# Splitting fp32 weights chunk by chunk in place of half by half, in a transformer layer on one NeuronCore

## The reference, cut to what matters

```
ul = (xl * (1 + sc1_l) + sh1_l) @ w_in          # 2048 x 13824, context likewise
y  = (gated linear recurrence, mean pooling, windowed attention)(uc, ul)
z  = sum over 3 branches of sigmoid(gates) * (y_j @ w_branch_j)
xl = layer_norm(ALPHA * xl + g1 * (z @ w_out))
xl = layer_norm(ALPHA * xl + g2 * (square(relu(mod(xl) @ w_ff1)) @ w_ff2))
```

## Time and profile before

| | |
|---|---|
| median of 3 runs | 1952.09 us (1946.99 to 1952.15) |
| profiled execution, whole | 1952.81 us |
| its span, first to last instruction | 1951.0 us |
| PE busy | 1885.7 us, 97% |
| DVE busy | 1258.3 us, 64% |
| ACT busy | 777.3 us, 40% |
| POOL busy | 389.3 us, 20% |
| mean granted clock of PE | 0.98 |
| read from HBM | 405.24 MB, 209 GB/s over the span |

### The profile page before, as it was taken

One profiled execution on the slowest core, in us unless ns is written; L12 is line 12 of the kernel. 1 busy time (PEld: TensorE's weight loads), 2 busy tenths in 40 slices (PEclk: granted clock), 3 DMA queues, 4 the chain that ended last, 5 costly groups with the idle time before them and its releaser, 6 DMA issues.

```text
span 1951.0 us, 26303 instructions
## 1 busy us (share of the span) xinstructions
PE 1885.7 (97%) x10808; PEld 1624.0 (83%) x10808; DVE 1258.3 (64%) x1438; ACT 777.3 (40%) x891; POOL 389.3 (20%) x325
## 2 busy tenths in 40 slices
PE   5999999999999999999999998999999999999996
PEld 1568887889999877887888887998998899889985
DVE  1247646786877776487676666766676467556686
ACT  1132224455555554444444435433333333333331
POOL 0000000002837343100010100450054024203500
PEclk7889999999999999999999999999999999999998
DMA  9957745555343454476676754666665566556652
GB/s 400 421 200 271 261 170 173 173 177 188 111 142 106 136 212 159 143 275 221 232 273 235 273 199 168 219 221 203 244 236 197 196 214 235 194 194 224 230 175 84
DMA packets 59319, 409.04 MB, mean 210 GB/s; under 512 B 6336, under 2 KB 9024, under 8 KB 10304
## 3 DMA queue, kind: packets, MB, share of 16 engines
q1 hardware_dynamic: 54720, 395.34, 57.2%
q10 hardware_dynamic: 4480, 12.02, 1.6%
HBM read 405.24 MB, written 2.10 MB: 209 GB/s over the span
## 4 chain that ended last, share of the span: by engine, by line
PE 86%; DVE 7%; DMA 2%; POOL 1%; DVEq 1%; issue 1%; ACT 1%; SPq 0%; ACTq 0%
PE main L1324 14%; PE main L1326 14%; PE main L1325 14%; PE main L1285 11%; PE main L1286 11%; PE main L1287 11%; DVE asum L868 2%; DMA raw<-in_w_ada 2%; PE main L1375 2%; DVE wlo L847 2%; PE main L1376 2%; PE main L1377 2%; PE side L1356 1%; PE side L1519 1%; PE side L1589 1%
## 5 line engine op out<-in xcount | busy, mean ns | idle before, releaser
L847 DVE TENSOR_TENSOR wlo<-raw,whi 128x1024 fp32r<-128x1024 f32 x552 | 722.3, 1334 | 329.8 <-ACT whi L405 329.2
L405 ACT CAST whi<-raw 128x1024 fp32r<-128x1024 f32 x552 | 574.1, 1050 | 792.8 <-PE main L1326 421.3
L1285 PE MATMUL main<-h,whi 128*128 128x256 f32 x1024 | 291.5, 285 | 4.6 <-DVE h L1180 2.5
L1286 PE MATMUL main<-h,whi 128*128 128x256 f32 x1024 | 291.1, 284 | 0.0
L1287 PE MATMUL main<-h,wlo 128*128 128x256 f32 x1024 | 291.0, 284 | 0.0
L1285 PE MATMUL main<-hCL,whi 128*128 128x256 f32 (+1 forms) x800 | 261.9, 327 | 7.1 <-DVE ya L1030 3.6
L1286 PE MATMUL main<-hCL,whi 128*128 128x256 f32 (+1 forms) x800 | 258.4, 323 | 0.0
L1287 PE MATMUL main<-hCL,wlo 128*128 128x256 f32 (+1 forms) x800 | 258.2, 323 | 0.0
L868 DVE SCALAR_TENSOR_TENSOR asum<-raw,sm,asum 128x512 f32<-128x512 f32 x240 | 192.6, 802 | 19.5 <-issue 0.4
L1324 PE MATMUL main<-whi,hid 128*128 128x512 f32 x512 | 201.2, 393 | 0.9 <-DVE wlo L847 0.9
L1285 PEld LDWEIGHTS main<-h,whi 128*128 128x128 f32 x1024 | 197.8, 193 | 5.1 <-DVE h L1180 2.8
(11 more groups left out here) (226 smaller groups left out, 2631.2 us busy)
## 6 DMA issues: line engine op xcount, KB each, us to landing
raw<-in_w_f SPq DMA_DIRECT2D x128, 1024.0 KB, 4.9
raw<-in_w_in SPq DMA_DIRECT2D x108, 1024.0 KB, 4.9
raw<-in_w_ada SPq DMA_DIRECT2D x96, 1024.0 KB, 6.2
raw<-in_w_br SPq DMA_DIRECT2D x24, 1024.0 KB, 5.0
raw<-in_w_out SPq DMA_DIRECT2D x16, 1024.0 KB, 5.0
xin<-in_xT SPq DMA_DIRECT2D x4, 1024.0 KB, 18.2
ax<-in_xtok ACTq DMA_DIRECT2D x1, 2048.0 KB, 8.4
lng<-in_rows ACTq DMA_DIRECT2D x2, 1024.0 KB, 7.1
```

The lines of the kernel that those rows point to most:

```text
L405: nc.scalar.copy(whi[:, q % 4], slots[slot][:, 2 * h:2 * h + 2]).then_inc(hi_made, 1)
L847: TT(wlo[:, q % 4], slots[slot][:, 2 * h:2 * h + 2], whi[:, q % 4].bitcast(F32), ALU.subtract).then_inc(lo_made, 1)
L1285: mm(out, w_hi, x_hi, start=start, stop=False)
L1286: mm(out, w_hi, x_lo, start=False, stop=False)
```

## The change

A call of `split` for a whole chunk now issues one instruction on ACT and one on DVE, each over 128 x 2048 elements, into two neighbouring places of `whi` and `wlo`. ACT waits once, for both halves of the chunk before the last, and each engine raises its semaphore by 2 at the end. The first chunk of the MLP is still called with one half at a time, and goes through the old code. The memory is the same.

```diff
@@ ScalarE
             def split(name, n, halves=(0, 1)):
                 slot = ST.slot(name, n)
                 act.wait_ge(raw_full[slot], ST.full(name, n))
+                if len(halves) == 2:
+                    q = ST.half(name, n, 0)
+                    if q >= 4:
+                        which, count = PN.last[q - 3]
+                        act.wait_ge(ended[which], count)
+                    nc.scalar.copy(whi[:, q % 4:q % 4 + 2].rearrange("p a b c -> p (a b) c"),
+                                   slots[slot][:]).then_inc(hi_made, 2)
+                    return
                 for h in halves:
                     q = ST.half(name, n, h)
@@ VectorE
             def split(name, n, halves=(0, 1)):
                 slot = ST.slot(name, n)
+                if len(halves) == 2:
+                    q = ST.half(name, n, 0)
+                    dve.wait_ge(hi_made, q + 2)
+                    hi, lo = (w[:, q % 4:q % 4 + 2].rearrange("p a b c -> p (a b) c") for w in (whi, wlo))
+                    TT(lo, slots[slot][:], hi.bitcast(F32), ALU.subtract).then_inc(lo_made, 2)
+                    return
                 for h in halves:
```

## The result

The changed kernel took 1978.41 us (median of 4 runs, 1977.10 to 1978.97), the one before, on the same chip, 1949.54 us (4 runs, 1945.81 to 1952.15): a ratio of 1.0155, 95% interval 1.0135 to 1.0176, 28.9 us longer. The forecast was 1970.4 us, 18.3 longer. The profiled execution took 1978.81 us, its span is 1977.0.

A forecast was written before the change was run, and what follows sets the result against it. PE was taken as the bound, 97% busy, so work off DVE or ACT counts only where PE waits. Terms 5.7 + 4.6 + 0.5 + 3.7 + 4.1 + 0.2 - 0.5 = 18.3 us gave 1970.4 us, range 1960 to 1987.

The forecast's parts named there:

- likeliest case: Whole kernel: the summed losses give 1970.4 us, 18.3 longer, within 1965 to 1976; chance 0.60.
- rival 1: Splits beside POOL: contention grows with instruction length, 4.5 us per chunk, 26.4 us longer in all, 1979 us; chance 0.20.
- rival 2: PE's clock: new stands could bring it down again, 1.5 to 5 us each, three such 1978 us; chance 0.07.
- Opening: Three opening chunks: PE waits for cast and subtraction, 4.37 us where it was 2.46; 5.7 us in all.
- Beside POOL: Levels and attention: one turn with POOL, 3.4 us per whole chunk; 0.2 us lost at levels, 4.1 in attention.
- the levels keep their cover but for 0.2 us: Recurrence levels, 24 chunks mostly 7.5 us on PE: the later split stays hidden except for 0.2 us.
- the exponentials of the levels had more than 0.9 us to spare: Levels, on ACT: exponentials behind the later cast come 0.9 us later, but had more slack, so no cost.
- the rotation beside chunk 17: Attention, beside gates chunk 17: a 0.8 us loss, part of the attention's 4.1.
- Fed by the first half: After pooling 1.4 us, at the MLP's start 1.05, in the last quarter 1.05 twice: 4.6 us.
- Tails: Last chunks of the output projection and the MLP: PE stands 1.85 us at each, 3.7 us in all.
- Small ones: Three places after out_rows that just miss, 0.5 us lost; forget stage, where DVE sets the end, 0.5 gained.
- Rival 3: DVE: saved fixed cost and fewer turns with POOL make the kernel faster, 1946 us; chance 0.05.

The follow-up runs named there:

- experiment 1: Kernel before, with only the four chunks of the opening split whole, all others in halves: 1955.17 us, ratio 1.0046 to the kernel before.
- experiment 12: Kernel before with first halves of opening chunks quartered and cast before the sums' copy, plus level chunks and first 24 gates chunks whole: 1952.39 us.
- experiment 6: Kernel before, with DVE subtracting whole chunks while ACT still casts halves: 1971.07 us, ratio 1.0124 to the kernel before.
- experiment 5: Kernel before, with ACT casting whole chunks while DVE still subtracts halves: 1971.16 us, ratio 1.0127 to the kernel before.
- experiment 2: Changed kernel, with the opening split in halves as before and everything else whole: 1971.63 us, ratio 1.0132 to the kernel before.
- experiment 4: Changed kernel, with the last chunks of the output projection and of the MLP in halves: 1971.76 us, ratio 1.0141 to the kernel before.
- experiment 11: Changed kernel, with the opening's first halves quartered and cast before the copy of the sums: 1966.72 us.
- experiment 9: Kernel before, with ACT casting the first half of opening chunks before copying out the sums: 1943.40 us, ratio 0.9989.

## Why the prediction was right, and where it wasn't

The direction, the mechanism and the range held: a whole chunk is ready 4.7 us after PE has left its place (4.57 forecast), steady chunks cover it, opening, tails and tight chunks don't. The likeliest case didn't hold as a number: it had 1965 to 1976, and 1978.4 lies beside it, at the 1979 of rival 1 and the 1978 of rival 2. By the time alone rival 1 would have been chosen, and its mechanism is false; the cost was 28.9 us where the sum had 18.3, and the time is only 8.0 off because the kernel before has a median of 1949.5 here and had 1952.1 there. Five terms were mis-sized.

- **Opening: 5.7 us forecast, 9 measured, 4.9 to 12.8** (experiment 1). The stands came as written, 9.0 to 15.0 us in all. The step that failed is the one that wrote the clock beside the stand as if a longer stand changed nothing in it. I had the row of the 0.52 and took it for a cost that both kernels pay; before pays it in some of its runs, and every profile with stands of 5.0 us has paid it in part or in full. Two profiles could not show that, since the run of before that was profiled had paid it. That the clock makes the difference is shown by the windows of single profiles and by 36 runs with shorter stands, not by a profile of each run.
- **Beside POOL: 4.3 us forecast, 7 to 9 measured** (experiment 12). The price of a collision was right as one turn with POOL's instruction, though not always 3.4 us: the 23 wholes that lost over 0.3 us took 2.7 to 4.5. The turn grows with POOL's instruction, and a whole that began behind one of 128x1024 took 4.48, rival 1's number but not its mechanism, with the same 2.2 us on top as a half. The whole subtraction at 713.38 took 2.47 us, that at 781.55 3.44, and POOL's L783 4.42 where it took 3.36 beside a half; the excess was 24 and 29 us for wholes (the change, experiment 6) and 61 and 56 for halves (before, experiment 5). Rival 1, that it grows with the length, falls. What failed is that the levels keep their cover but for 0.2 us, and that the exponentials of the levels had more than 0.9 us to spare. At two levels POOL is itself held up one turn, and its last level releases ACT's exponential, behind which the ya copies stand that PE waits for. At two others POOL is idle, and the later subtraction holds up DVE's masked copy. Each of the four is 0.9 us. And the rotation beside chunk 17, 0.8 in the forecast, was 1.05, and 1.42 of lower clock in the profile of the change (none in experiment 12).
- **Fed by the first half: 4.6 forecast, 6.7 measured.** The one at the end of the pooling came exactly (1.4). In the last quarter it was 1.6 and 1.3 where I wrote 1.05: I had taken DVE's start as fixed, and at the first of them it came 0.6 us later. At the MLP's start the stand grew by only 0.2 us, but 0.9 came one chunk earlier and 1.5 after it, by the clock.
- **Tails: 3.7 forecast, 5.6 measured.** 2.1 for each against 1.85, and 1.4 of lower clock in the second, which experiment 2 does not have. The trace of experiment 4 gives the sum back.
- **Small ones: 0.5 and -0.5 forecast, 1.0 and +0.2 measured, 2.4 not forecast.** The latency of 0.27 + 1.91 + 0.10 + 2.29 + 0.14 = 4.71 us in place of 4.57 uses up the margin at places that just missed. The gain in the forget stage did not show.

Rival 2, the clock, had 0.07 as a case of its own. It was right beside the forecast, not in its place: in the profile of the change gates 17, the MLP's fourth chunk and its tail carry 1.4 + 1.5 + 1.4 = 4.3 us, and the opening 9 - 5.7 = 3.3, with the wide interval of experiment 1. It should have been a term of the sum with a price and a chance at each new stand. Rival 3 fell: the fixed cost and over half the collisions went, 62.7 us off DVE, and PE did not see it.

The Trainium skill (SBUF — State Buffer, section on who interferes with whom) states the port pair of the two engines as an exclusive lock. By that rule one collision costs one turn; the trace agrees, with 2.20 us on top of a half and 2.19 on top of a whole beside the same POOL instruction.

## What to carry to other kernels

Halves are not overhead where the consumer can start on the first one: count an instruction's fixed cost (here 0.16 us a chunk on DVE, never seen by PE) against the latency that the whole adds to the first use (here 1.9 us), and ask at openings, tails and behind busy queues, not in the steady loop. A stand of PE is priced with what comes after it, so look at the granted clock in the window behind each stand, and at whether the spread of the run times has two groups, before a single profile is taken as the kernel's. And where two engines hold each other up by whole instructions, as DVE and POOL do here, a longer instruction meets fewer of the other's but holds each of them up longer, and what waits behind it on a third engine gets later.

## What was not expected of the hardware

- With the same code and stands of 3.0 us, PE ran the next nine microseconds at a granted clock of 0.50 in one profile and of 1.00 in another, 9.3 us apart at the fourth chunk. With stands of 5.0 us no profile was of the short kind. With one of 3.0 and two near 2.0, or with all three near 2.0 or less, none of 36 runs was in the upper group. The short kind has low stretches too: 0.89 of the clock from 46 to 54 us and 0.71 from 100 to 110 in experiment 9.
- Stands of 1.85 to 2.5 us in the middle of dense work (mean granted clock 0.99 from 705 to 1240 us) were followed by 2 to 5 us at 0.51 to 0.69 of the clock, while one of 2.05 us in the kernel before, at the MLP's fourth chunk, was not (5.82 us for the chunk against 7.31). The same stand can go either way: 2.46 us at gates 17 was followed by a fall in the change and experiments 2, 4, 6 and 11 and not in 12, and 1.85 us in the MLP's tail in the change and experiment 11 and not in 2.
- A DVE subtraction of 1.22 us and one of 2.29 both took 2.2 us longer beside a POOL instruction over 128x1024 (3.42 and 4.48 us).
- DVE starts 0.10 us after the end of a cast of 128x2048, and 0.03 after one of 128x1024 (medians of the 204 and 212 for which it waited). In the second MLP matrix ACT's cast starts 0.28 us after PE has begun the next chunk; before, it was 0.20 after the next half.
